# First mixer's head norms: squares of two row halves added, high and low part stacked, one product with ones per sum

## The reference

```
def rms_norm(x, gain):
    xf = x.astype(jnp.float32)
    y = xf * lax.rsqrt(jnp.mean(xf * xf, axis=-1, keepdims=True) + EPS)
    return (y * gain.astype(jnp.float32)).astype(x.dtype)

# dilated_mixer
qkv = (h @ w_qkv).reshape(B, S, 3, N_GROUPS, A_HEADS, A_HEAD_DIM)
for g, (window, dil) in enumerate(DIL_CONFIGS):
    q = rope(rms_norm(qkv[:, :, 0, g], q_gain[g]), S)
    k = rope(rms_norm(qkv[:, :, 1, g], k_gain[g]), S)
```

## Time and profile before

| | |
|---|---|
| median of 3 runs | 2912.12 us (2911.56 to 2912.29) |
| span of the profiled execution | 2915.0 us |
| TensorE busy | 2883.1 us, 99% of the span, 13308 matmuls |
| ScalarE, VectorE, GpSimd busy | 1622.2, 1104.5, 407.5 us |
| granted TensorE clock | 1.000 over the span |

### The profile page before, as it was taken

How to read it: one execution, slowest core, us unless ns; L and a number is a source line. 1 busy time by engine, 2 the same in 40 slices (tenths; PEclk the granted TensorE clock), 3 DMA queues, 4 the chain that set the end, 5 groups by cost and what they waited for, 6 DMA issues and landing times.

```text
span 2915.0 us, 35588 instructions
## 1 busy us (share of the span) xinstructions
PE 2883.1 (99%) x13308; PEld 2374.8 (81%) x13308; DVE 1104.5 (38%) x2221; ACT 1622.2 (56%) x2410; POOL 407.5 (14%) x472
## 2 busy tenths in 40 slices
PE   9999999999999999999999999999999999999999
PEld 7989889888887678888887887888877788788887
DVE  6554736211214754111225214423244611642235
ACT  7675767544445755444456545545455644654554
POOL 1111111111111001111110111111111011111110
PEclk9999999999999999999999999999999999999999
DMA  8676867788887318988895797888878488788884
GB/s 247 152 160 137 178 134 162 165 192 194 193 194 154 87 40 200 196 192 194 193 195 117 155 193 164 199 191 195 184 182 187 92 182 193 168 187 191 202 191 116
DMA packets 137004, 499.11 MB, mean 171 GB/s; under 512 B 15344, under 2 KB 15600, under 8 KB 136720
## 3 DMA queue, kind: packets, MB, share of 16 engines
q0 software_dynamic: 67296, 245.59, 47.7%
q1 hardware_dynamic: 68688, 249.59, 28.2%
q10 hardware_dynamic: 864, 1.78, 0.2%
HBM read 494.81 MB, written 2.10 MB: 170 GB/s over the span
## 4 chain that ended last, share of the span: by engine, by line
PE 91%; ACT 3%; DVE 3%; DMA 1%; issue 1%; DVEq 1%; ACTq 0%
PE ps L1136 73%; PE ps L1155 5%; PE ps L1495 3%; DMA wl<-weights 1%; PE ps L1255 1%; PE ps L1436 1%; PE ps L1417 1%; PE ps L1418 1%; PE ps L1642 1%; DVE arena L2312 1%; ACT arena L1007 1%; PE ps L1216 0%; PE ps L1238 0%; PE ps L1620 0%; PE ps L1356 0%
## 5 line engine op out<-in xcount | busy, mean ns | idle before, releaser
L468 ACT ACTIVATE wh<-raw 128x1024 fp32r<-128x1024 f32 (+1 forms) x465 | 489.8, 1053 | 934.8 <-PE ps L1136 902.1
L1136 PE MATMUL ps<-HH,wh 128*128 128x512 f32 x2224 | 870.8, 392 | 5.3 <-DVE HL L2255 2.1
L1136 PE MATMUL ps<-HH,wl 128*128 128x512 f32 x2224 | 865.8, 389 | 0.0
L1136 PE MATMUL ps<-HL,wh 128*128 128x512 f32 x2224 | 865.7, 389 | 0.0
L452 POOL DMA_DIRECT2D wl<-weights x465 | 405.6, 872 | 2472.2 <-ACT wl L472 2472.0
L1136 PEld LDWEIGHTS ps<-HH,wh 128*128 128x128 f32 x2224 | 417.5, 188 | 98.0 <-issue 8.6
L1136 PEld LDWEIGHTS ps<-HL,wh 128*128 128x128 f32 x2224 | 417.5, 188 | 87.3 <-issue 1.4
L1136 PEld LDWEIGHTS ps<-HH,wl 128*128 128x128 f32 x2224 | 417.4, 188 | 87.3
L472 ACT ACTIVATE wl<-raw 128x1024 fp32r<-128x1024 f32 (+1 forms) x465 | 483.7, 1040 | 0.0
L1136 PE MATMUL ps<-MH,wh 128*128 128x512 f32 x1056 | 412.0, 390 | 1.0 <-DVE ML L2135 0.7
L1136 PE MATMUL ps<-MH,wl 128*128 128x512 f32 x1056 | 410.9, 389 | 0.0
(11 more groups left out here) (331 smaller groups left out, 3007.4 us busy)
## 6 DMA issues: line engine op xcount, KB each, us to landing
raw<-weights SPq DMA_DIRECT2D x468, 512.0 KB, 5.5
wl<-weights POOLq DMA_DIRECT2D x465, 512.0 KB, 7.8
XT<-x SPq DMA_DIRECT2D x4, 512.0 KB, 8.3
out<-XT SPq DMA_DIRECT2D x3, 512.0 KB, 2.7
arena<-tables POOLq DMA_DIRECT2D x1, 1024.0 KB, 11.1
arena<-table_h ACTq DMA_DIRECT2D x1, 640.0 KB, 5.6
arena<-swaps_a POOLq DMA_DIRECT2D x1, 576.0 KB, 8.7
out<-XT SPq DMA_DIRECT2D x2, 256.0 KB, 2.4
```

The lines of the kernel that those rows point to most:

```text
L468: act_f(wh[:, n, 0:w], raw[:, n, 0:w], ACT.Copy)
L1136: op = mm(bank(g, t), w[:, slot, at:at + P], x[:, first + kt, :], start=(kt == 0 and w is wh and x is xh), stop=(kt == n_k - 1 and w is wl ...
```

## The change

Each pair of tiles is now squared once, in two instructions of 64 partitions by 1024 elements: one squares the lower 64 features of both tiles, one the upper 64 and writes them to the same 64 partitions. VectorE adds the two (`a_join`). ScalarE rounds the sum into one half of the partitions of a stack (`a_square_high`), and VectorE writes the low part into the other half (`a_lows`). One product of ones with the stack then sums high and low together. Tiles 0 and 1 of a set use partitions 0 to 63 of `sq`, tiles 2 and 3 partitions 64 to 127, and each has its own stack (`MH[:, 6:8]` or `ML[:, 6:8]`). The two copies to `qk` become one. The sums are placed one step later, after kt = 2 and kt = 4. In VectorE's queue the join of tiles 0 and 1 stands ahead of tile 3 (and 7) of the rotation, and their low part behind it, with the join and the low part of tiles 2 and 3.

```diff
@@ scalar
-            def a_squares(n, tiles_in, first):
-                for t in (first, first + 1):
-                    add_waits(act, sq_used, n, t - 1)
-                    act_f(sq[:, t, :], tiles_in(t), ACT.Square)
-                    act_f(sq_hi[:, t % 2, :], tiles_in(t), ACT.Square).then_inc(sq_ready, 1)
+            def a_squares(src, first):
+                rows, _ = stacked_rows(first)
+                act_f(sq[rows, 0:2, :], src[0:64], ACT.Square)
+                act_f(sq[rows, 2:4, :], src[64:P], ACT.Square).then_inc(sq_ready, 2)
 
             def a_copies(g, tset, first):
-                for t in (first, first + 1):
-                    act_f(qk[:, 4 * tset + t, :], bank(g, t), ACT.Copy).then_inc(qk_kept, 1)
+                b = 4 * g.mod(2) + first
+                act_f(qk[:, 4 * tset + first:4 * tset + first + 2, :], ps[:, b:b + 2, :], ACT.Copy).then_inc(qk_kept, 2)
+
+            def a_square_high(n, first):
+                rows, _ = stacked_rows(first)
+                act.wait_ge(sq_joined, n.div(2).value(1 + first // 2))
+                act_f(sq_stack[first // 2][rows, :, :], sq[rows, 0:2, :], ACT.Copy).then_inc(sq_high, 1)
 
             def a_results(g, tset, last, between):
-                n = c.take("sq", 4)
+                n, k = c.take("sq", 4), c.take("join", 4)
                 wait_used(act, last)
-                a_squares(n, lambda t: bank(g, t), 0)
+                b = 4 * g.mod(2)
+                a_squares(ps[:, b:b + 2, :], 0)
                 a_copies(g, tset, 0)
+                a_square_high(k, 0)
                 between()
-                a_squares(n, lambda t: bank(g, t), 2)
+                a_squares(ps[:, b + 2:b + 4, :], 2)
                 a_copies(g, tset, 2)
+                a_square_high(k, 2)
@@ tensor
-                if kt not in (1, 3):
+                if kt not in (2, 4):
                     return
-                for t in (kt - 1, kt):
+                for t in (kt - 2, kt - 1):
...
-                    pe.wait_ge(sq_low, 4 * k + t + 1)
-                    mm(bank(g, t), ones_r[:, :], sq_hi[:, t % 2, :], start=True, stop=False)
-                    mm(bank(g, t), ones_r[:, :], sq_lo[:, t % 2, :], start=False, stop=True).then_inc(sq_used, 1)
+                    pe.wait_ge(sq_low, 2 * k + t // 2 + 1)
+                    mm(bank(g, t), ones_r[:, :], sq_stack[t // 2][:, t % 2, :], start=True, stop=True).then_inc(sq_used, 1)
@@ vector
-            def a_lows(n, first):
-                for t in (first, first + 1):
-                    dve.wait_ge(sq_ready, (n + t).value(1))
-                    v.tensor_tensor(sq_lo[:, t % 2, :], sq[:, t, :], sq_hi[:, t % 2, :], ALU.subtract).then_inc(sq_low, 1)
+            def a_join(n, first):
+                rows, _ = stacked_rows(first)
+                dve.wait_ge(sq_ready, (n + first).value(2))
+                v.tensor_tensor(sq[rows, 0:2, :], sq[rows, 0:2, :], sq[rows, 2:4, :], ALU.add).then_inc(sq_joined, 1)
+
+            def a_lows(k, first):
+                rows, other = stacked_rows(first)
+                dve.wait_ge(sq_high, (k + first).div(2).value(1))
+                dve.drain()
+                v.tensor_tensor(sq_stack[first // 2][other, :, :], sq[rows, 0:2, :], sq_stack[first // 2][rows, :, :],
+                                ALU.subtract).then_inc(sq_low, 1)
@@ vector, first_norm (pair 0)
-                a_lows(lows, 0)
+                a_join(squares, 0)
+                a_lows(joined, 0)
                 split(2, scaled(4), hf, parts(HH, HL, 4))
-                a_lows(lows, 2)
+                a_join(squares, 2)
+                a_lows(joined, 2)
                 split(2, scaled(6), hf, parts(HH, HL, 6))
@@ vector, a_pair
                 for t in range(11):
                     if t in (3, 7):
-                        a_lows(n + (t + 1), 0)
+                        a_join(n + (t + 1), 0)
                     a_tile(t, q + t)
                     if t in (3, 7):
-                        a_lows(n + (t + 1), 2)
+                        a_lows(k + (t + 1), 0)
+                        a_join(n + (t + 1), 2)
+                        a_lows(k + (t + 1), 2)
```

More of the change, by code:

```diff
@@ L71 @@
 N_LALL = N_LPAR + 2 * P
-A_PAIR = dict(slab=18, group=6, sq=12, qk=12)
+A_PAIR = dict(slab=18, group=6, sq=12, qk=12, join=12)
 M_STEPS, M_PER = 32, 8
@@ L127 @@
 class Counts:
-    NAMES = ("slab", "group", "split", "sq", "qk", "att", "ts", "hl", "ln", "up", "pre")
+    NAMES = ("slab", "group", "split", "sq", "qk", "att", "ts", "hl", "ln", "up", "pre", "join")
     def __init__(self):
@@ L230, in block_program @@
         sq = tiles3(7, NSQ)
-        sq_hi, sq_lo = MH[:, 6:8, :], ML[:, 6:8, :]
+        sq_stack = (MH[:, 6:8, :], ML[:, 6:8, :])
         rs = tiles3(11, 4)
@@ L310, in block_program @@
         sq_low, qk_kept, ones_ready = sem("sq_low"), sem("qk_kept"), sem("ones_ready")
+        sq_joined, sq_high = sem("sq_joined"), sem("sq_high")
         ts_ready = sem("ts_ready")
@@ L390, in a_out, with stacked_rows @@
             return bank(g, 2 + hd)
+        def stacked_rows(first):
+            rows = slice(0, 64) if first == 0 else slice(64, P)
+            return rows, slice(64, P) if first == 0 else slice(0, 64)
         def m_scores(j):
@@ L557, in a_first @@
                 high_parts(s + (SLOTS + 2), 1)
+                k = c.take("join", 4)
                 act.wait_ge(q_first, 2)
-                a_squares(n, lambda t: qk[:, t, :], 0)
+                a_squares(qk[:, 0:2, :], 0)
+                a_square_high(k, 0)
                 high_parts(s + (SLOTS + 3), 1)
@@ L563, in a_first @@
                 act.wait_ge(q_first, 4)
-                a_squares(n, lambda t: qk[:, t, :], 2)
+                a_squares(qk[:, 2:4, :], 2)
+                a_square_high(k, 2)
                 new_high(6)
@@ L609, in exp_row @@
                 return e
-            def a_squares(n, tiles_in, first):
-                for t in (first, first + 1):
-                    add_waits(act, sq_used, n, t - 1)
-                    act_f(sq[:, t, :], tiles_in(t), ACT.Square)
-                    act_f(sq_hi[:, t % 2, :], tiles_in(t), ACT.Square).then_inc(sq_ready, 1)
-            def a_copies(g, tset, first):
-                for t in (first, first + 1):
-                    act_f(qk[:, 4 * tset + t, :], bank(g, t), ACT.Copy).then_inc(qk_kept, 1)
+            def a_squares(src, first):
+                rows, _ = stacked_rows(first)
+                act_f(sq[rows, 0:2, :], src[0:64], ACT.Square)
+                act_f(sq[rows, 2:4, :], src[64:P], ACT.Square).then_inc(sq_ready, 2)
+            def a_copies(g, tset, first):
+                b = 4 * g.mod(2) + first
[4 more added lines that the diff above has]
+                act_f(sq_stack[first // 2][rows, :, :], sq[rows, 0:2, :], ACT.Copy).then_inc(sq_high, 1)
             def a_results(g, tset, last, between):
-                n = c.take("sq", 4)
+                n, k = c.take("sq", 4), c.take("join", 4)
                 wait_used(act, last)
-                a_squares(n, lambda t: bank(g, t), 0)
+                b = 4 * g.mod(2)
+                a_squares(ps[:, b:b + 2, :], 0)
                 a_copies(g, tset, 0)
+                a_square_high(k, 0)
                 between()
-                a_squares(n, lambda t: bank(g, t), 2)
+                a_squares(ps[:, b + 2:b + 4, :], 2)
                 a_copies(g, tset, 2)
+                a_square_high(k, 2)
                 return n
@@ L1189, in a_sums @@
             def a_sums(g, k, kt):
-                if kt not in (1, 3):
+                if kt not in (2, 4):
                     return
-                for t in (kt - 1, kt):
+                for t in (kt - 2, kt - 1):
                     if k:
-                        pe.wait_ge(qk_kept, 4 * k + t - 3)
-                    pe.wait_ge(sq_low, 4 * k + t + 1)
-                    mm(bank(g, t), ones_r[:, :], sq_hi[:, t % 2, :], start=True, stop=False)
-                    mm(bank(g, t), ones_r[:, :], sq_lo[:, t % 2, :], start=False, stop=True).then_inc(sq_used, 1)
+                        pe.wait_ge(qk_kept, 4 * k + 2 * (t // 2) - 2)
+                    pe.wait_ge(sq_low, 2 * k + t // 2 + 1)
+                    mm(bank(g, t), ones_r[:, :], sq_stack[t // 2][:, t % 2, :], start=True, stop=True).then_inc(sq_used, 1)
             def a_scores(g, pair, hd, q):
@@ L1744, in first_norm @@
                     v.tensor_tensor(qk[:, t, :], bank(g, t), rs_first, ALU.mult).then_inc(q_first, 1)
-                lows = c.at["sq"]
-                a_lows(lows, 0)
+                squares, joined = c.at["sq"], c.at["join"]
+                a_join(squares, 0)
+                a_lows(joined, 0)
                 split(2, scaled(4), hf, parts(HH, HL, 4))
-                a_lows(lows, 2)
+                a_join(squares, 2)
+                a_lows(joined, 2)
                 split(2, scaled(6), hf, parts(HH, HL, 6))
@@ L1902, in a_pair @@
                 g = gs + 1
-                n = c.take("sq", 12)
```

(13 more changed lines are left out.)

## The result

The changed kernel takes 2925.13 us (median of 4 runs, 2923.07 to 2927.77) against 2912.2 us before (4 runs, 2911.56 to 2913.59): 12.9 us longer, a ratio of 1.004 with a 95% interval of 1.0029 to 1.0052. The forecast was 2924.5. All numbers here are of fast executions; one of experiment 4, of 10312 us at a granted clock of 0.38, is left out.

A forecast was written before the change was run, and what follows sets the result against it. TensorE was taken as the only bound of the changed stage. Pair 0 at 8.7 us slower plus three pairs at 1.2 slower (3.7) gave 12.4 on the 2912.1 median: 2924.5 us, +0.4%, range 2912 to 2932.

The forecast's parts named there:

- Removed: TensorE: 12 sum products a pair go, 48 in all, saving 2.8 us a pair, 11.3 us in four pairs.
- Prices: New half-width instructions: 1.03 us per ScalarE square, 0.95 for copy and rounding, 1.225 per VectorE join or low part.
- The low bounds: Lowest prices allowed: 0.9 us on ScalarE, 1.1 on VectorE, no loss at a change of partition half; +4 in sum.
- the waits just eat the gain: Rival, no change: lowest prices, pairs 1 to 3 at -0.7 each, pair 0 at +6; +4, 2916; chance 0.2.
- the saving that I worked out from it: ScalarE half set by the skill's table: only 0.6 us more in place of 1.1, sum some 5 us lower.
- Second sets: Pairs 1 to 3: both sums ready, no wait; `a_rms` at 12.75, tile 0 at 14.8 into the set.
- Third and value sets: TensorE waits at the sum for the low part behind a rotation tile: 1.5 us in the third, 1.4 in value.
- Second head's scores: TensorE waits 0.9 us there because tile 11 ends 9.8 after the value set, scores due at 9.05.
- Pair 0: First pair: waits of 1.1, 1.9, 3.6, 3.2, 1.4 and 0.9 us, restarts, less savings: 8.7 us slower.
- not additive: Slab 8's DMA wait, 3.6 us: were the slab in time, TensorE would wait longer for the low part.
- Sums never late: Rival, faster: join ahead of tile 3 starts by 2.0 into the set; -8, at most -11, 2902 to 2904; chance 0.1.
- Late weights everywhere: Rival, slower still: slab landings 2 to 3 us over median, nine sets lose about 1 us each, 2933; chance 0.15 with high prices.

The follow-up runs named there:

- experiment 4: Kernel before, with only the sum product of ones with the low part left out: 2902.92 us, ratio 0.9969.
- experiment 1: Changed kernel with the sums one step later again, after kt = 3 and kt = 5: 2932.03 us, ratio 1.0068.
- experiment 2: Changed kernel with the low part of tiles 0 and 1 directly behind their join, ahead of rotation tile 3 (and 7): 2940.03 us, ratio 1.0096.
- experiment 6: Changed kernel with `a_rms` of tiles 0 and 1 ahead of the next set's first slab in ScalarE's queue: 2920.02 us, ratio 1.0024.
- experiment 7: Changed kernel with one of VectorE's five instructions of each rotation tile left out: 2908.69 us, ratio 0.9987.
- experiment 5: Changed kernel with the sums back at their old places, after kt = 1 and kt = 3: 2953.67 us, ratio 1.0142.

## Why the prediction was right

**Removed:** forecast 11.3. Experiment 4 shows 11.2 by the starts of the trace, 9.6 net. In the changed kernel a set without waits takes 22.75 in place of 23.68, 11.2 over twelve sets.

**Prices:** 1.03 and 1.225 taken, 1.02 to 1.06 and 1.22 measured. The squares start 1.04 apart (292.95, then 293.99), the price that I took from the change of partition half in the earlier trace rows. The low bounds, and with them the rival in which the waits just eat the gain, fall with that.

The Trainium skill, "VectorE: DVE Perf Modes", section on the TRN2 errata, counts one fixed cost per instruction and advises larger tiles. The trace agrees on the price of one (its estimate for 1024 columns from PSUM is 1.00, measured 1.02), but not on the saving that I worked out from it: with `a_rms` at 12.86 the extra delay of the half sets is that of the rows. For an instruction stream what counts is the distance of starts, and before the change that was 0.48 for squares 0.60 long.

**Second sets:** no wait in pairs 1 to 3, as forecast.

**Third and value sets:** forecast waits 1.5 and 1.4; by the starts of the products TensorE loses 1.8 and 1.5 (1.62 and 1.30 of idle in the rows above, and the restart).

**Second head's scores:** forecast 0.9, measured 0.5 (0.2 of idle and the restart). Together the three make 3.8 against 3.8 to 4.0, and a pair costs 1.0 against 1.2. The total of a pair is nearer than its terms.

**Pair 0:** forecast 8.7, lag 9.0, and here the agreement is luck in good part. By stages the forecast has 4.7 to the start of the third set, 2.3 in it, 0.5 in the value set and 0.9 at the second head's scores (0.3 for restarts beside them). The lags show 4.4, 4.6, -0.3 and 0.3. The first is right, though one term of it was too high: the wait for slab 8 was 2.55 and not 3.6, and of the 1.1 ahead of the first sum 0.82 stood at a slab. The wait of the third set's sum was 3.89 and not 3.2, the part that I had called not additive. Behind it, in the value set, TensorE waited 0.37 and not 1.4. TensorE of the changed kernel, second and third set of pair 0:

```profile
50.37 0.74 PE L1217 MATMUL ps<-ML,ones_r 128*128 128x512 f32 x2 [1.80 <-DVE ML L1726]
...
61.84 0.47 PE L1156 MATMUL ps<-HH,wh 128*128 128x512 f32 x1 [2.55 <-DMA wl<-weights]
...
74.18 1.19 PE L1217 MATMUL ps<-MH,ones_r 128*128 128x512 f32 x2 [3.89 <-DVE MH L1726]
75.17 0.63 PE L1156 MATMUL ps<-HH,wh 128*128 128x512 f32 x1
75.60 0.63 PE L1156 MATMUL ps<-HL,wh 128*128 128x512 f32 x1
```

And one term was missing. Behind the wait of 3.89 the two sums take 0.99 in place of 0.53, and the next five products start 0.43 apart and not 0.227, at granted clock 0.50: from 74.18 to 77.65 that is 1.6 us more than at the full clock.

**What I had not seen** is how the terms hang together. The sum treated each wait as a loss of its place; I did carry the slip from set to set, and so the total came out. But a list of waits invites experiments 1 and 2 as mends, and both make the kernel slower.

**Rivals.** Sums never late: refuted by the 13.1 us; its condition was a join by 2.0 into the third set, and it starts at 3.67. Late weights everywhere: absent in the changed kernel, where after pair 0 no weight is waited for, but it is what stopped experiment 6.

## What to carry to other kernels

When several engines hand a tile round in a fixed order, add up one whole round (each engine's queue positions, not its busy time) and compare it with the time of the engine that bounds the kernel. If the round is longer, a wait can be moved but not removed; shorten the round or reorder the queues. Here 48 matmuls less were worth nothing until that was done, with ScalarE and VectorE busy for only 92 and 72 of 130 us in the stage. And two instructions of half the partitions cost twice one of all (1.02 us each on ScalarE, 1.03 for all): folding rows saves TensorE, and charges ScalarE and VectorE full price.

## What the runs showed of the hardware that I had not expected

After some of its waits TensorE goes on at the lower of its two clock levels. In the changed kernel this is so behind the wait of 3.89 us, which follows 8 us of products without a gap: the granted clock is 0.50 for the next 2 us. It is not so behind those of 2.55, 1.80 and 1.62, where it stays at 1.00. But the length of the wait alone doesn't tell. The first window below is the one behind 3.89. The next two are of experiment 2, behind two waits of 2.59 at the same place of pairs 2 and 3. Then come one of experiment 7 behind a wait of 2.48, and one of experiment 1 behind a wait of 3.03:

```profile
75.20:77.20 2.00, 2.00 (x6) 1.62 (x5) 0.81 (x2) 1.74 (x3) 0.00 (x0) 0.50 0.80 133
...
383.80:387.80 4.00, 4.00 (x17) 3.83 (x18) 1.42 (x8) 2.08 (x8) 0.73 (x1) 0.63 0.79 180
512.95:516.95 4.00, 4.00 (x29) 3.89 (x30) 2.50 (x15) 2.38 (x11) 0.73 (x1) 1.00 0.76 176
...
61.60:66.00 4.40, 4.34 (x12) 3.46 (x13) 4.24 (x6) 4.20 (x5) 0.86 (x1) 0.61 0.95 188
...
61.40:64.00 2.60, 2.54 (x11) 2.17 (x12) 2.50 (x5) 2.59 (x4) 0.64 (x1) 1.00 0.91 136
```

The shortest wait with the lower clock behind it is 1.79 us (experiment 6), the longest without is 3.26 (experiment 5). What decides between them no run here shows. The cost, read from the starts, was most often 1.6 us, and 2.9 behind the last wait of experiment 1.

So a wait is not always paid at face value: of two ways to distribute the same lateness, the one with many short waits (changed kernel, 2925) beat the one with few long ones (experiment 1, 2932), and 6.3 us of the difference are the clock's.

The Trainium skill, "TensorE: Matmul & The Clock Gate", says in its Part 1 that the engine's clock is set by how busy the engine has been recently. The traces agree in kind: 1.6 us lost in pair 0 of the changed kernel, 1.6 to 2.9 a pair in experiment 1.
